# Decoder step: the window keys' products of the sample moved from VectorE to GpSimd, behind its gathers

## The reference, cut to what matters

```
s_past = einsum('bqgrd,bqgkld->bqgrkl', qg, kv_sel[..., 0, :]) * scale   # selected rows
s_w    = einsum('bqgrd,bsgd->bqgrs',   qg, kv_w[:, :, 0]) * scale       # window rows
p_w    = _masked_softmax(s_w, ...)
o_w    = einsum('bqgrs,bsgd->bqgrd', p_w, kv_w[:, :, 1])
```

## Time and profile before

| | us |
|---|---|
| median of 3 runs | 1491.34 |
| lowest and highest | 1487.87 to 1501.76 |
| profiled execution, its own time | 1485.38 |
| its span, first to last instruction | 1483.6 |
| steps 0 to 7 in the span | 803 to 1374 |

### The profile page before, as it was taken

The page is one execution under the profiler, slowest core; times in us unless marked ns, Lnnn a source line. Parts: engine busy times, 40 slices in busy tenths (PEclk is TensorE's granted clock), DMA queues, the critical chain, the costliest instruction groups (busy, mean ns, idle before and its releaser), DMA issues. The chain is left out here.

```text
span 1483.6 us, 27692 instructions
## 1 busy us (share of the span) xinstructions
PE 1246.0 (84%) x10087; PEld 861.8 (58%) x10087; DVE 799.3 (54%) x1190; ACT 254.5 (17%) x714; POOL 176.4 (12%) x153
## 2 busy tenths in 40 slices
PE   0899853999999676998887998889897979797995
PEld 0899842888788564555554885546453546354331
DVE  2355112078999963336664537484949485735022
ACT  0111114111211110224443110101010101100113
POOL 0000000020000000000002205142332315040000
PEclk9999985999999955579999999898998999998898
DMA  8988225257878753200003839698979798766850
GB/s 216 264 253 250 59 78 188 90 165 225 276 263 278 246 120 127 116 1 1 1 1 97 267 103 307 213 291 261 302 227 302 241 309 273 260 208 205 287 205 29
DMA packets 206021, 282.08 MB, mean 190 GB/s; under 512 B 21933, under 2 KB 126918, under 8 KB 205438
## 3 DMA queue, kind: packets, MB, share of 16 engines
q1 hardware_dynamic: 110078, 202.47, 40.7%
q10 hardware_dynamic: 89376, 60.01, 14.1%
q0 software_dynamic: 6432, 17.83, 3.8%
HBM read 273.32 MB, written 11.11 MB: 192 GB/s over the span
## 5 line engine op out<-in xcount | busy, mean ns | idle before, releaser
L1594 PE MATMUL bank<-xnT,e_wg 128*128 128x260 f32 x1152 | 273.5, 395 | 0.5 <-DMA e_wg<-in_w_in 0.5
L1594 PEld LDWEIGHTS bank<-xnT,e_wg 128*128 128x128 f32 x1152 | 222.8, 196 | 75.0 <-issue 29.6
L598 PE MATMUL score_banks<-xnT,oT 128*128 128x260 f32 (+1 forms) x864 | 197.1, 386 | 8.7 <-DMA oT<-in_w_in 8.7
L1578 POOL DMA_INDIRECT d_slc<-in_cache_nsa_slc,selrow x128 | 157.7, 1232 | 373.8 <-PE score_banks L1665 330.2
L598 PEld LDWEIGHTS score_banks<-xnT,oT 128*128 128x128 f32 (+1 forms) x864 | 161.5, 189 | 38.7 <-DMA oT<-in_w_in 9.0
L234 PE MATMUL score_banks<-c_cols,c_w 64*64 64x64 f32 (+1 forms) x4096 | 130.1, 222 | 44.6 <-DMA c_w<-in_w_cmp 35.0
L234 PEld LDWEIGHTS score_banks<-c_cols,c_w 64*64 64x64 f32 x4096 | 126.4, 138 | 48.3 <-issue 48.1
L1602 PE MATMUL bank<-oT,e_wb 128*128 128x512 f32 x192 | 100.0, 669 | 20.0 <-DVE mt L1856 10.5
L273 DVE COPY c_cols<-c_page 128x1024 f32<-128x1024 f32 x48 | 49.5, 1130 | 88.4 <-DMA c_page<-in_cache_nsa_cmp 88.4
L1627 PE MATMUL bank<-d_vpage,d_pf 128*8 128x512 f32 x512 | 80.8, 644 | 18.6 <-DMA d_vpage<-in_cache_fox_kv 18.6
L1305 DVE TENSOR_REDUCE f_nm<-score_banks 128x2 f32<-128x512 f32 (+3 forms) x56 | 45.0, 804 | 81.2 <-PE score_banks L1256 80.3
(11 more groups left out here) (367 smaller groups left out, 1455.2 us busy)
## 6 DMA issues: line engine op xcount, KB each, us to landing
d_vpage<-in_cache_fox_kv SPq DMA_DIRECT2D x256, 256.0 KB, 4.8
d_kpage<-in_cache_fox_kv SPq DMA_DIRECT2D x96, 256.0 KB, 5.7
oT<-in_cache_fox_kv SPq DMA_DIRECT2D x80, 256.0 KB, 3.7
mt<-in_cache_fox_kv SPq DMA_DIRECT2D x80, 256.0 KB, 3.7
e_wg<-in_w_in ACTq DMA_DIRECT2D x36, 512.0 KB, 6.2
c_page<-in_cache_nsa_cmp SPq DMA_DIRECT2D x128, 128.0 KB, 3.6
oT<-in_w_in ACTq DMA_DIRECT2D x13, 1024.0 KB, 8.1
c_page<-in_cache_nsa_cmp ACTq DMA_DIRECT2D x64, 128.0 KB, 3.6
```

The lines of the kernel that those rows point to most:

```text
L598: last = nc.tensor.matmul(pj[ch.n % 2][i][0:ch.w, 0:NM if ch.mem else TH], w[:, c, ch.off:ch.off + ch.w], rhs, start=c == 0, stop=c == DC - 1)
L1578: nc.gpsimd.indirect_dma_start(out=slc[:, n, :], out_offset=None, in_=k.cache_slc, in_offset=bass.IndirectOffsetOnAxis(ap=k.selrow[:, at:a ...
L1594: last = nc.tensor.matmul(gate_bank[n % 2][:, 0:TH], wg[product % WR][:, c, :], k.xnT[:, c, part * TH:(part + 1) * TH], start=c == 0, stop ...
```

## The change

The addresses of a small product become a function of their own, `small_operands`. The window's two products of a step leave VectorE: GpSimd issues them after the step's 16 gathers, once the query row and the window are there, and counts them in the same `small_times`. VectorE still issues the selected products, and all sums.

```diff
+        def small_operands(kind, g, n):
+
+            tiles = NWIN if kind == "win" else 8
+            feats = slice(g * HD, (g + 1) * HD)
+            keys = win[:, :, feats] if kind == "win" else slc[:, g * 8:g * 8 + 8, feats]
+            at = (n % 2) * 2048
+            product = scratch[:, at:at + R * tiles * HD].rearrange("p (r n d) -> p r n d", r=R, n=tiles)
+            rows = qrows_of["nsa"][:, g * R * HD:(g + 1) * R * HD].rearrange("p (r d) -> p r d", r=R)
+            return product, keys.unsqueeze(1).to_broadcast([P, R, tiles, HD]), rows.unsqueeze(2).to_broadcast([P, R, tiles, HD])
+
...
                             bounds_check=POOL * P - 1, oob_is_err=False).then_inc(slc_in, 16)
+                    pool.wait_ge(q_in, event["nsa", b] + 1)
+                    pool.wait_ge(win_in, (b + 1) * 16)
+                    for g in range(G):
+                        product, keys, rows = small_operands("win", g, b * 4 + g)
+                        after(pool, small_scored, b * 4 + g - 1)
+                        nc.gpsimd.tensor_tensor(product, keys, rows, ALU.mult).then_inc(small_times, 1)
...
-                    feats = slice(g * HD, (g + 1) * HD)
...
-                    nc.vector.tensor_tensor(product, keys.unsqueeze(1).to_broadcast([P, R, tiles, HD]),
-                                            rows.unsqueeze(2).to_broadcast([P, R, tiles, HD]), ALU.mult).then_inc(small_times, 1)
+                    product, keys, rows = small_operands(kind, g, n)
+                    if kind == "slc":
+                        nc.vector.tensor_tensor(product, keys, rows, ALU.mult).then_inc(small_times, 1)
                     ve.wait_ge(small_times, n + 1)
```

## The result

The changed kernel takes **1524.78 us** (median of 4 runs, 1522.96 to 1529.61), the kernel before 1493.49 (4 runs). The ratio is 1.021, 95% interval 1.0155 to 1.0265, so the change costs 23 to 40 us. Forecast were 1525 and a loss of 34.4.

The account below looks back on a forecast made before the run. VectorE's string from query row to maxima was taken to bound steps 1 to 7; their losses sum to +34.4 us, 1485.38 to 1519.8, or 1525 us on the runs' median scale, range 1508 to 1558.

Parts of the forecast that it names:

- VectorE's string is the path in steps 1 to 7: A microsecond added to VectorE between query row and maxima is a microsecond on the path in these steps.
- The sign that I named: TensorE's wait for the maxima, 18.9 us before, was to grow by 20 us or more.
- rival 4: No loss: the delay vanishes in TensorE's 16.4 us of waits for value pages; 1491 us, chance 0.04.
- The last gather comes after VectorE's arrival: In every step the last gather ends 2 to 16 us after VectorE reaches the window products.
- Rival 2: Slow POOL product of 4.2 us, operands broadcast and stepped: each step gains 3.5, +24 us, 1550; chance 0.07.
- Rivals 1 and 3: Product waits for POOL's closing DRAIN (1555, chance 0.14); POOL changes program between gather and product (1572, chance 0.06).
- G + 6.6: Second window sum's end after last gather's end G: 0.30 gap, two products of 2.45, sum 1.22, handovers 0.2.
- How the gathers move: Eleven gathers in steps 1 to 7, lengthened by VectorE products, lose that lengthening: 9.3 us.
- Step 0 costs nothing: TensorE's merge sets step 0's pace; VectorE waited 34.2 us there, so a 3 us delay is made up.
- The step list: Losses forecast for steps 1 to 7: 5.2, 3.1, 4.3, 6.6, 4.3, 6.8, 4.1 us; sum 34.4.
- The gap of step 7: POOL's 6.75 us gap, taken for instruction fetching; if longer code moves it into a wait, 1518 us.
- rival 5: Faster: with gathers done before VectorE reaches the window, it saves 2.4 us a step, -17 us, 1474; chance 0.03.

Follow-up runs that it names:

- experiment 2: Changed kernel with each GpSimd window product issued twice, the second behind the first by a semaphore: 1554.79 us, ratio 1.0427.
- experiment 1: Kernel before, window products still on VectorE, the first waiting for a GpSimd mark behind the step's last gather: 1513.0 us, ratio 1.015.
- experiment 6: Kernel before with a semaphore per group's 8 gathers, and steps 2 to 6's window products on GpSimd after 4 gathers: 1464.44 us, ratio 0.9834.
- the four executions with unchanged steps: Traces of the kernel before and the three kernels of experiment 7; steps 1 to 7 and tail take 597.6, 601.3, 598.0 and 605.2 us.
- experiment 7: Three kernels: kernel before with 1 or 8 more gathers ahead of step 0, or 40 memsets behind the last gathers: ratios 1.001, 1.0008, 1.0004.
- experiment 4: Changed kernel with each step's two window products issued after 8 of its 16 gathers instead of behind all: 1515.1 us, ratio 1.0152.

## Why the prediction was right

- *VectorE's string is the path in steps 1 to 7.* Right: experiment 2 passes 30 to 32 of 33 us on. The sign that I named was half wrong: the wait for the maxima grew by 12.5 us only (18.9 to 31.4), not 20 or more. The other waits of TensorE on VectorE, for the merge products that stand behind the window sums, grew by as much each: 10.5 to 23.0 for `mt`, 9.5 to 20.9 for `cst`. In these steps TensorE feels the delay already there. The waits for value pages, in which rival 4 let the delay vanish, fell from 16.4 to 9.4, so they took in a part of it at most; the four changes add up to 29.4 us.
- *The last gather comes after VectorE's arrival.* Right in all eight steps; experiment 1 prices it at 22 of 31 us, with 9 to 36 by its interval.
- *Duration of a product.* 2.45 taken, 2.36 measured (4.66 for two in a row). Rival 2 is out: with operands that are broadcast and stepped the product takes less than the 2.54 that the plain 128x520 row gives in proportion.
- *The gap ahead of the product.* 0.30 taken from the gathers, 0.01 measured. Rivals 1 and 3 are out with it: POOL's closing DRAIN doesn't mean that a product waits, and no change of program stands between. With both terms right, the sums end at G + 5.9 instead of G + 6.6, and the sum of the steps would have come out 5 us lower, at 29.5.
- *How the gathers move.* 9.3 us taken for steps 1 to 7; all 128 gathers together took 145.2 us instead of 157.7, 12.5 less. By the Trainium skill ("SBUF — State Buffer", section "Who interferes with whom") a tensor_tensor doesn't stall descriptor generation. The rows are against it once more: in experiment 6 the gather of 1033.97, begun inside a page product, took 2.51 instead of 1.00.
- *Step 0 costs nothing.* It lost 1.1 us ((898.32 - 814.88) - (886.03 - 803.67)).
- *The step list.* 34.4 forecast, 31.6 measured, no step off by more than 1.7 us, which is closer than unchanged steps agree among themselves. With the two terms right the list would have said 29.5, and the 2 us to the measured sum lie within the same scatter. TensorE's matmuls in steps 1 to 6 took 375 us, against 369 to 374 in the four executions with unchanged steps, at a mean granted clock of 0.89 of full speed against 0.92 in each of the four; how much of that lies on the path isn't shown.
- *The total.* That it came out within 1 us of 1525 is luck in part: two terms were 5 us too high, the loss of 31.3 is 3 below the 34.4, and the kernel before had a median of 1493.5 in these runs, 2 above the 1491.3 that the forecast counts from.
- *The gap of step 7* as a fetch of code, a side remark of rival 5, is not borne out (experiment 7): the gap was still 6.69 us with POOL's longer code.

## What to carry to other kernels

An engine that is idle 88% of the time is no place to put work without asking when in its queue the work comes: compare the end of what stands ahead of it with the moment at which the other engine arrives, step by step. Work by which two engines shut each other out (experiment 4) has to be placed where the other engine waits or does work that isn't held up, as the sums weren't: beside POOL's second product a sum kept its 1.22 us. And before work is moved, look whether a wait can be cut finer; here that alone brought about twice what the best placed move added.

## What the runs showed of the hardware that I had not expected

- A VectorE product that meets two GpSimd products in a row doesn't get in between them: 5.42 us instead of 2.28 when it began 1.4 us into the pair (experiment 4), and up to 6.55 in step 6 of the same kernel, where it began 0.26 us into the pair.
- Between a gather and a product that follows it POOL stands idle for 0.01 us in step 3, between two gathers for 0.30.
- There is a gap of 6.6 to 7.5 us ahead of the second gather of the last step, with 1 or 8 more gathers ahead of it and with 40 memsets behind it too, and of 2.26 where the gathers count in two semaphores.
